# Input projection by Strassen's scheme: seven block products for each pair of feature tiles, in place of eight

## What is computed

```python
z = x @ w_in + b_in                        # 512 x 2048 by 2048 x 14352
glu_val, glu_gate, gate_c, q, k, v, f_logit, gate_a = split(z)   # 2048 columns each, f_logit 16
u = glu_val * sigmoid(glu_gate)
c = causal_depthwise_conv(u, w_dw, 31 taps) + b_dw
y_conv = silu(layer_norm(c)) * silu(gate_c)
cum = cumsum(log_sigmoid(f_logit))
p = softmax(q k^T / sqrt(128) + cum_q - cum_k, causal)           # 16 heads of 128
y_attn = (p v) * silu(gate_a)
out = layer_norm(2**0.25 * x + [y_conv, y_attn] @ w_out + b_out)
```

## Time and profile before

| | |
|---|---|
| time, median of 3 runs | 1765.31 us |
| profiled execution, its span | 1763.0 us |
| TensorE busy with matmuls | 1733.5 us, 98% of the span, 7644 matmuls |
| VectorE busy | 1071.8 us, 61% |
| ScalarE busy | 539.6 us, 31% |
| GpSimd busy | 215.4 us, 12% |
| DMA, mean rate | 101 GB/s |

### The profile page before, as it was taken

The page is one execution under the profiler, slowest core; times in us unless marked ns, Lnnn a source line. Parts: engine busy times, 40 slices in busy tenths (PEclk is TensorE's granted clock), DMA queues, the critical chain, the costliest instruction groups (busy, mean ns, idle before and its releaser), DMA issues. The chain is left out here.

```text
span 1763.0 us, 21898 instructions
## 1 busy us (share of the span) xinstructions
PE 1733.5 (98%) x7644; PEld 1400.0 (79%) x7644; DVE 1071.8 (61%) x1669; ACT 539.6 (31%) x791; POOL 215.4 (12%) x176
## 2 busy tenths in 40 slices
PE   7999999999999999999999999999999999999997
PEld 5888888888888888888888888888688877788885
DVE  4356757667586575765857657577754565344347
ACT  4323223222232232223223232232544432222240
POOL 0120101201012010110111101100200044000000
PEclk8999999999999999999999999999999999999999
DMA  5333342333323433333333333333233333332232
GB/s 157 109 110 87 95 110 71 110 97 94 100 73 108 105 91 96 77 104 110 95 92 77 108 100 95 98 83 86 70 108 96 119 131 132 124 115 95 95 120 96
DMA packets 259691, 178.09 MB, mean 101 GB/s; under 512 B 8193, under 2 KB 246945, under 8 KB 258737
## 3 DMA queue, kind: packets, MB, share of 16 engines
q1 hardware_dynamic: 258656, 170.39, 33.6%
q0 software_dynamic: 1008, 7.34, 1.2%
HBM read 173.48 MB, written 4.23 MB: 101 GB/s over the span
## 5 line engine op out<-in xcount | busy, mean ns | idle before, releaser
L635 PE MATMUL ps<-xh,wh 128*128 128x512 f32 x1792 | 716.4, 400 | 0.7 <-DVE wl L876 0.7
L636 PE MATMUL ps<-xl,wh 128*128 128x512 f32 x1792 | 711.9, 397 | 0.0
L637 PE MATMUL ps<-xh,wl 128*128 128x512 f32 x1792 | 711.5, 397 | 0.0
L876 DVE TENSOR_TENSOR wl<-raw,wh 128x1024 fp32r<-128x1024 f32 x280 | 370.3, 1324 | 391.0 <-ACT wh L388 387.1
L635 PEld LDWEIGHTS ps<-xh,wh 128*128 128x128 f32 x1792 | 338.8, 189 | 81.5 <-DVE wl L876 0.8
L637 PEld LDWEIGHTS ps<-xh,wl 128*128 128x128 f32 x1792 | 338.4, 189 | 81.8
L636 PEld LDWEIGHTS ps<-xl,wh 128*128 128x128 f32 x1792 | 338.9, 189 | 80.1 <-issue 0.5
L388 ACT ACTIVATE wh<-raw 128x1024 fp32r<-128x1024 f32 x280 | 288.2, 1054 | 297.0 <-PE ps L637 221.8
L921 DVE SCALAR_TENSOR_TENSOR y<-u,taps,y 128x512 f32 (+1 forms) x240 | 193.6, 807 | 0.0
L921 DVE SCALAR_TENSOR_TENSOR odd<-u,taps,odd 128x512 f32<-128x512 f32 x224 | 186.6, 833 | 0.0
L635 PE MATMUL ps<-wh,yh 128*128 128x512 f32 x464 | 183.0, 394 | 3.1 <-DVE yl L1162 3.1
(11 more groups left out here) (167 smaller groups left out, 1068.3 us busy)
## 6 DMA issues: line engine op xcount, KB each, us to landing
raw<-in_w_in_dram SPq DMA_DIRECT2D x224, 512.0 KB, 3.7
raw<-in_w_out_dram SPq DMA_DIRECT2D x64, 512.0 KB, 3.6
probs<-forget_sums_dram SPq DMA_DIRECT2D x16, 256.0 KB, 7.4
res<-in_x_dram POOLq DMA_DIRECT2D x4, 1024.0 KB, 5.3
out_dram<-res SPq DMA_DIRECT2D x8, 512.0 KB, 2.7
probs<-forget_sums_dram SPq DMA_DIRECT2D x16, 192.0 KB, 6.2
probs<-forget_sums_dram SPq DMA_DIRECT2D x16, 128.0 KB, 4.8
y<-in_x_dram SPq DMA_DIRECT2D x2, 768.0 KB, 9.0
```

Source lines behind the costliest of these rows:

```text
L635: nc.tensor.matmul(o, ah, bh, start=start, stop=False, skip_group_check=True)
L636: nc.tensor.matmul(o, ah, bl, start=False, stop=False, skip_group_check=True)
L637: return nc.tensor.matmul(o, al, bh, start=False, stop=True, skip_group_check=True)
L876: vec.tensor_tensor(wl[:, 2 * par + h, :], raw[:, h, :], wh[:, 2 * par + h, :], ALU.subtract) \
```

## The change

Two feature tiles A and B are now made together, in a group. The 2048 rows of `w_in` are halved and the 512 tokens are halved, and the 2 x 2 block product is done by Strassen's scheme in Winograd's form with 7 block products in place of 8. A unit is one such product: 8 blocks of 128 rows, three matmuls each, 24 matmuls of 256 columns. There are 56 groups and 392 units.

- Weights: four blocks (B11, B12, B22, B21) are loaded for a group, as much data as before, into a ring of seven 512 KB buffers. Three sums of blocks are made per group: `sum_1` (B11 + B12) on GpSimd, `sum_2` (sum_1 + B22) on VectorE, and two in place by an accumulating DMA that GpSimd issues, `sum_3` (B12 + B22) and `sum_4` (the second sum and B21). Each of the 7 units has its own `high` on ScalarE and `low` on VectorE, 7 in place of 8 for two tiles, into three slots.
- x: each of the 8 row blocks becomes seven factor blocks of 256 tokens (`xh`, `xl` of shape 7 x 8 x 256), made at the start by four additions on VectorE (`x_sums`), one rounding and one subtraction.
- Results: the products of a group gather in four PSUM banks, and three ScalarE and five VectorE instructions of 256 columns (`evict`) put the two tiles together in SBUF (`tiles`).
- Attention: q and k are split from SBUF, the probabilities are scaled on ScalarE, and the term of the softmax that is constant along a row is left out, so that only the mask is added on GpSimd.
- Convolution: the taps go into one accumulator in PSUM, each waiting for the tap before it.
- Room: attention tiles, conv tiles and output gates are written to DRAM and read back for the layer norm (`cin`) and for the output projection (`ya_0`, `ya_1`, `yc`, `z_slot`). The conv branch is normalised in the first 17 steps of the output projection.
- All loops over heads, tiles and steps are written out as straight code.

```diff
+ORDER = (1, 2, 4, 5, 6, 7, 3)
+GROUPS = HEAD_GROUPS + HEADS // 2
+UNITS = 7 * GROUPS
+SOURCE = {1: B11, 2: B21, 3: B22, 4: SUM, 5: SUM, 6: SUM, 7: B12}
+TAPS_AT = ((1, 0, 1, 2, 1, 2, 2), (2, 1, 1, 2, 2, 2, 2), (0, 1, 2, 2, 2, 2, 1))
...
+            def loads(g):
+
+                if g >= 2:
+                    sp.wait_ge(t4_in[g % 2], parity(g - 2))
+                load_block(g, B11, 0, 0)
+                if g >= 2:
+                    sp.wait_ge(low_done, at(g - 2, 4) + 1)
+                load_block(g, B12, 0, 1)
+                if g >= 1:
+                    sp.wait_ge(low_done, at(g - 1, 1) + 1)
+                    sp.wait_ge(t1_done, g)
+                load_block(g, B22, 1, 1)
+                if g >= 1:
+                    sp.wait_ge(low_done, at(g - 1, 7) + 1)
+                load_block(g, B21, 1, 0)
...
+            def sum_1(g):
...
+                nc.gpsimd.tensor_tensor(raw[:, ring(g, SUM), :], raw[:, ring(g, B11), :], raw[:, ring(g, B12), :],
+                                        ALU.add).then_inc(t1_done, 1)
+
+            def sum_3(g):
+
+                pool.wait_ge(t1_done, g + 1)
+                pool.wait_ge(block_in[B22][g % 2], parity(g))
+                nc.gpsimd.dma_start(raw[:, ring(g, B12), :], raw[:, ring(g, B22), :], accum_op=ALU.add) \
+                  .then_inc(t3_in[g % 2], 16)
+
+            def sum_4(g):
+
+                pool.wait_ge(low_done, at(g, 6) + 1)
+                pool.wait_ge(block_in[B21][g % 2], parity(g))
+                nc.gpsimd.dma_start(raw[:, ring(g, SUM), :], raw[:, ring(g, B21), :], accum_op=ALU.add) \
+                  .then_inc(t4_in[g % 2], 16)
...
+            for k in range(HALF + 1):
+                if k < HALF:
+                    x_copy(k)
+                if k >= 1:
+                    x_high(k - 1)
...
+            def product(n, k):
+
+                g, m = UNIT_OF[n]
+                a = slice(P * k, P * (k + 1))
+                f = FACTOR[m]
+                return mm3(ps[:, BANK_OF[m], 0:TOK], w_high(n)[:, a], w_low(n)[:, a], xh[:, f, k, :], xl[:, f, k, :],
+                           k == 0 and m in (1, 2, 5, 7))
...
+            def sum_2(g):
+
+                dve.wait_ge(low_done, at(g, 5) + 1)
+                dve.wait_ge(block_in[B22][g % 2], parity(g))
+                o = raw[:, ring(g, SUM), :]
+                vec.tensor_tensor(o, o, raw[:, ring(g, B22), :], ALU.add).then_inc(t2_done, 1)
...
+                    dve.wait_ge(tap_done, i * (TAPS - 1) + w)
+                    if w < TAPS - 1:
+                        vec.scalar_tensor_tensor(out=o, in0=u[:, w:w + SEQ], scalar=tap, in1=o,
+                                                 op0=ALU.mult, op1=ALU.add).then_inc(tap_done, 1)
...
+            for g in range(GROUPS):
+                for s in range(7):
+                    n = slot_unit(g, s)
+                    i, count = convs(g, s)
+                    before = 0 if g % 3 == 0 and s == 4 else count // 2
+                    conv(i, before)
+                    if n is not None:
+                        low(n + 2)
+                        if n + 2 < UNITS and UNIT_OF[n + 2][1] == 5:
+                            sum_2(UNIT_OF[n + 2][0])
...
+                    evict(g, s)
+                    attention(g, s)
+                    conv(i, count - before)
```

More of the change, by code:

```diff
@@ L61 @@
+PT_LEN = 1280
+PR_AT = [P * i * (i + 1) // 2 for i in range(NT + 1)]
+OUT_STEPS = 64
+PER_PASS = 32
 END = 8
 E0 = OUT_STEPS - END
-VAL, GLU, GATE_C, Q, K, V, GATE_A = range(7)
-F_COL = 6 * D
[L67 to L75, removed]
+FIN = 8
@@ L90, in sem @@
             return ctx.enter_context(nc.semaphore(name))
[L93 to L102, removed]
+        over = ExitStack()
@@ L169, in build @@
[L169 to L180, removed]
@@ new lines, in end_y, with bias @@
+        def end_y(ring_y, last, end, q):
+            return last[:, q, :] if q < 4 else ring_y[:, q % 2, :] if q < 6 else end[:, q - 6, :]
+        def bias(table, kind, i):
+            return table[:, kind * HEADS + i:kind * HEADS + i + 1]
+        x_loaded = [sem(f"x_loaded{n}") for n in range(len(X_CUTS))]
+        f_loaded, rows_loaded, fbias_loaded, dw_loaded = (sem("f_loaded"), sem("rows_loaded"), sem("fbias_loaded"),
+                                                          sem("dw_loaded"))
@@ L215, in build, with load_block @@
         stats_done, scaled_done = sem("stats_done"), sem("scaled_done")
         block = ctx.enter_context(nc.Block())
-        def ds(i, n):
-            return bass.ds(i, n)
         @block.sync
         def _(sp):
[L225 to L239, removed]
+            def load_block(g, block, half, tile):
+                kind, i = kinds_of(g)[tile]
+                c = col_of(kind, i)
+                sp.dma_start(raw[:, ring(g, block), :].rearrange("p (k c) -> p k c", k=HALF),
+                             w_in[1024 * half:1024 * (half + 1), c:c + P].rearrange("(k p) c -> p k c", p=P)) \
+                  .then_inc(block_in[block][g % 2], 16)
@@ new lines, in _ @@
+            for g in range(GROUPS):
+                sum_1(g)
+                sum_3(g)
+                if g < HEAD_GROUPS and g % 3 == 1:
+                    masks(g // 3)
+                sum_4(g)
+                if g < HEAD_GROUPS and g % 3 == 0 and g >= 6:
+                    add_conv(g // 3 - 2)
+                if g == HEAD_GROUPS:
+                    add_conv(HEADS - 2)
+                if g == HEAD_GROUPS + 2:
+                    add_conv(HEADS - 1)
+                if HEAD_GROUPS + 3 <= g < HEAD_GROUPS + 7:
+                    for j in range(4):
+                        add_square(4 * (g - HEAD_GROUPS - 3) + j)
@@ L1116, in _ @@
[L1116 to L1125 removed]
+                vec.tensor_scalar(neg_cum[0:HEADS, :], fcum, -1.0 / SCALE, None, ALU.mult).then_inc(f_vec, 1)
+                vec.memset(csum[:, :], 0.0).then_inc(vec_const, 1)
```

1729 lines of the change are left out of this document (939 added, 790 removed).

## The result

The changed kernel takes 1815.38 us (median of 4 runs, 1804.75 to 1824.88); the kernel before, run beside it, 1764.88 (4 runs, 1764.43 to 1766.93). The ratio is 1.0285, interval 1.0243 to 1.0328: **slower, by 50 us**, where 92 us less were forecast.

What follows compares the result with a forecast made beforehand. VectorE, at 67.2 us a head against TensorE's 65.2, was to bound the 16 heads; start 52, 48 groups 1071.5, gate groups 167, output and tail 380 make 1670.5, plus 2.3 for the median: 1673 us, range 1632 to 1745.

Steps and rivals of the forecast that it cites:

- Two handoffs are new ... I take 0.2 and 0.6.: In each head, TensorE's waits for the low parts of q and of the probabilities: 0.2 and 0.6 us.
- The two sums: Time asked for per head: TensorE 65.2 us, VectorE 67.2 us; the larger was taken as the bound.
- Eight gate groups: 8 x 19.7 = 157.3, where VectorE has slack: Gate groups after the heads: 157.3 us, VectorE having slack except in the group with 18 taps; 167 with mean and variance.
- beside steps of 5.6 us that VectorE and ScalarE fill by at most 4.5: Output projection: stores of y and reloads cost nothing beside 5.6 us steps that VectorE and ScalarE fill by at most 4.5.
- the third rival: In the heads, GpSimd's additions stop VectorE for their whole length: 75.0 us a head, 1798 us; chance 0.09.
- TensorE's waits for `low` (about 2 us a head): Sign expected in the heads if the forecast held, with VectorE over 90% busy there.
- VectorE's price list: Per head, VectorE's instructions sum to 62.0 us, PSUM taps adding nothing; GpSimd's interference, masks, conv sum and handoffs add 5.2.
- ScalarE's load, DMA sums, loads and stores at nothing: Whole kernel: ScalarE about 35 of 67 us a head; transfers in time, `sum_4` read about 12 us later; no cost.
- The 0.117 pitch: Units: 256-column matmuls 0.117 us apart, half of 512 columns; 9408 of them take 1101 us, 157 less than before.
- The first: Rival for the heads: TensorE stays the bound, slots hide GpSimd, a head takes 65.2 us; 1641 us, chance 0.22.
- the second: Rival for the heads: chained PSUM taps cost VectorE 0.1 us more each, 3.1 a head; 1723 us, chance 0.24 with its like.
- The four rivals: TensorE bound (0.22), dearer VectorE taps (0.24 with its like), GpSimd additions stopping VectorE (0.09), short matmuls not halving (0.03).

Runs made afterwards that it cites:

- The first experiment: Changed kernel with the scores moved behind the seventh unit of their group and p v behind the fifth, one slot later each: 1723.95 us.
- the memset: Changed kernel with GpSimd's `sum_1` not computed, a memset that reads no SBUF filling its tile: 1748.85 us.
- The shift of the squares: Changed kernel with ScalarE's squares in four gate groups one slot later, GpSimd's additions of them regrouped around `sum_1`: 1790.22 us.
- the version with the three shifts: Changed kernel with scores and p v a slot later, conv-tile activations and gating a step later, squares a slot later: 1681.22 us, 0.952 of the kernel before.
- the memset version: Changed kernel with attention, output-step activations and gate-group squares all moved later, and `sum_1` replaced by a memset: 1654.15 us, 0.9366 of the kernel before.
- the cut kernel before: Kernel before the change with each 512-column projection matmul made as two of 256, 10752 in all: 1779.76 us, 1.0081 of the kernel before.

## Why the prediction was wrong

**The step that failed** is "Two handoffs are new ... I take 0.2 and 0.6." They measured 40.0 / 16 = 2.5 and 27.3 / 16 = 1.7 us a head, and the lower clock behind them cost about 2.0 more, which the working did not have. It worked out each handover from an idle VectorE (rounding, `low`, last part: 2.9 to 3.4 us after the slot's start). But the next paragraph forecast VectorE 92% busy (62.0 of 67.2): what is wanted at once of an engine that full comes after its backlog. At the scores two taps (1.45 us) and a `low` held by `sum_1` (1.06) stood ahead, at p v two taps, a `low` and two evictions. The share of `sum_1` is shown by the memset; that of the taps is read from the timeline, and no run varied it. The two sums were taken as rivals for the bound, the larger to win; a wait at a fixed point makes them partly add up. The first experiment shows it: with one more slot of slack the head falls to 67.05, and the 48 groups from 1153.4 to 1066.2 (forecast 1071.5).

**The second, for 41 us,** is "Eight gate groups: 8 x 19.7 = 157.3, where VectorE has slack". The slack is there (VectorE is 79% busy), but it doesn't count in a loop in which VectorE and ScalarE wait for each other inside one slot: centre, square, round, `low`. The shift of the squares, with GpSimd's regrouped, gave back 20 of the 41. The other 19 or so are still there in the version with the three shifts (186.2 us for this stage), where TensorE's waits in it come to 12.5: 6.6 for `low`, 4.0 for the last unit's L1211 (5.3 before), 1.9 for an eviction. What the rest is stays open. **The third, for 15 us,** is "beside steps of 5.6 us that VectorE and ScalarE fill by at most 4.5": true of their work, but the steps took 7.02 by the loop. With it broken, the stage came in 6 under the 380.

The prediction gave "slower" a chance of 0.10, 0.09 of it for the third rival. The sign named, "TensorE's waits for `low` (about 2 us a head)", did not come either: of 21.6 us, 20.0 lie in the gate groups.

**What was right.** The start (52.7 for 52). VectorE's price list: taps through PSUM at nothing, a `low` held just under 1 us for each `sum_1`, 67.1 us a head once the handovers have room. That 67.1 comes so near 67.2 is in part luck: VectorE is busy for 65.7 of it, and TensorE, priced 1.4 too low, for 66.2. ScalarE's load, DMA sums, loads and stores at nothing: from the first group on, TensorE's list of waits names none of them, though in the gate groups ScalarE's roundings waited 15.2 us for `sum_1` (behind the additions of squares on GpSimd) and 8.4 for sums by DMA, and some of TensorE's wait for `low` there may be theirs. The 0.117 pitch was 3% low, 36 us on TensorE's time; in heads that VectorE bounds most of it hid (the memset version's 65.8 has no waits, where the working had 64.4 without them).

**The rivals.** The third gave 1798, nearest to the time, and 75.0 a head (deciding from 73.0 on); 72.7 was measured. That it came near is luck, since its mechanism was not the one: it needs each `low` held for 2.4 us, and they were held for 0.98 at most in the mean. The Trainium skill's rule in "SBUF — State Buffer", section "Who interferes with whom" (the later one locked out for the whole instruction) agrees with the 2.28 us `low`, held to the end of the addition; since taps stand between, less than the whole length is lost. The first falls by the heads of 67.1 with VectorE 98% busy, the second by the taps' 750 ns. The four rivals have no wait that a late engine makes and the lower clock lengthens, though TensorE's two new waits stand in the prediction, as its smallest terms.

**One more sign.** The changed kernel's runs scatter over 20 us, the version with three shifts over 2. The scatter goes with the clock: the four runs of 1804.75, 1810.9, 1819.85 and 1824.88 us had a mean granted clock of 0.974, 0.970, 0.968 and 0.961. Its heads take from 70.6 to 74.9 us in one execution, by how many of their waits brought the clock down, those of the shifted versions 66.8 to 67.4 from the second on.

## What to carry to other kernels

When a change fills a second engine almost as full as the first, price each point at which one waits for the other from the engine's place in its own order, with its backlog, and not from the work alone; where the two meet at a fixed point, give it a slot of slack, which cost nothing here and was worth 91 us. Look for loops in which two half-idle engines alternate inside one step: their time is the sum of the links, and moving one link a step later took most of the loss away in the output steps. And a wait on TensorE costs more than its length if the granted clock falls with it.

## What the runs showed of the hardware

- A wait of 2.76 us at full clock was followed by about 6 us at the 1.2 GHz level (0.50, then 0.65 in the windows), matmuls 0.21 us apart in place of 0.12. Keeping TensorE busy with 16 and 12 dummy matmuls a head gave 34 us back. That 32 waits, 67 us in all, draw 75 us of lower clock after them I had not expected. Only 18 of the 32 did, and those of up to 1.7 us at the same points of the version with the memset never did; what decides it no run shows.
- Matmuls of 256 columns stand 120 ns apart in the units, but 117 in p v (in the version with the attention a slot later, at full clock), and 118.5 in the cut kernel before. The cause was not found; no run varied it by itself.
- An addition of 128x1024 on GpSimd takes 2.38 us beside taps and before a `low`, as worked out between two sizes (2.40), and 2.72 in the mean.
- A VectorE instruction with two operands in SBUF stands still for the rest of the GpSimd addition, taps with one operand in PSUM don't (1.54 us for two, within L502, as without it).
